# Keys and the sample's queries of a retention layer turned by VectorE blocks and DMAs instead of TensorE, in a two-layer streaming encoder

## The reference

```
z = rmsnorm(h) @ w_in                  -> u | gp | q | k | v | gr, 1024 columns each
qr = rotary(q) ; kr = rotary(k) / 16   (4 heads of 256)
per chunk: scores = qr @ kr.T * D
           o = scores @ v + (qr * q_decay) @ S
           S = S * chunk_decay + (kr * k_decay).T @ v
o = groupnorm(o) * g_gn * silu(gr)
h = h + concat(pool(u) * silu(gp), o) @ w_out
h = h + sigmoid(rmsnorm(h) @ w_pg) * (p @ w_ple) ; at the end rmsnorm(h)
```

## Time and profile before

| | us |
|---|---|
| median of 3 runs | 2436.83 |
| lowest, highest | 2434.78, 2438.3 |
| the profiled execution's own time | 2435.57 |
| its span | 2433.8 |
| PE busy in it | 2419.9 |
| DVE busy | 1059.6 |
| ACT busy | 635.7 |
| POOL busy | 300.0 |
| mean granted TensorE clock, share of full speed | 0.998 |

### The profile page before, as it was taken

How to read it: one execution, slowest core, us unless ns; L and a number is a source line. 1 busy time by engine, 2 the same in 40 slices (tenths; PEclk the granted TensorE clock), 3 DMA queues, 4 the chain that set the end, 5 groups by cost and what they waited for, 6 DMA issues and landing times.

```text
span 2433.8 us, 27213 instructions
## 1 busy us (share of the span) xinstructions
PE 2419.9 (99%) x11024; PEld 1994.5 (82%) x11024; DVE 1059.6 (44%) x1650; ACT 635.7 (26%) x994; POOL 300.0 (12%) x471
## 2 busy tenths in 40 slices
PE   9999999999999999999999999999999999999998
PEld 8888888888888888888888888888888888888886
DVE  6343443444455335444543433434434552354445
ACT  6212221221233223322432122122122231242222
POOL 2102102103112001000020120120130120010001
PEclk9999999999999999999999999999999999999999
DMA  7344244244244334223342442442442454332323
GB/s 233 99 124 137 81 131 136 81 123 152 86 130 155 109 100 128 81 76 120 103 160 78 134 135 78 124 137 87 118 154 80 131 162 122 109 112 78 95 70 113
DMA packets 187566, 283.73 MB, mean 117 GB/s; under 512 B 19024, under 2 KB 130960, under 8 KB 186160
## 3 DMA queue, kind: packets, MB, share of 16 engines
q1 hardware_dynamic: 143616, 173.05, 23.7%
q0 software_dynamic: 29824, 95.11, 12.5%
q10 hardware_dynamic: 14000, 13.83, 2.4%
HBM read 235.45 MB, written 46.46 MB: 116 GB/s over the span
## 4 chain that ended last, share of the span: by engine, by line
PE 98%; DVE 1%; DMA 0%; ACT 0%; issue 0%; SPq 0%; POOL 0%; DVEq 0%; POOLq 0%; ACTq 0%
PE acc L1567 89%; PE side L1567 8%; PE osb L1794 1%; DMA Z<-in_x_t 0%; PE side L1757 0%; DVE Wlo L971 0%; PE osb L1567 0%; DVE Z L1415 0%; DVE Alo L974 0%; PE side L1683 0%; DVE HT L1408 0%; DVE HT L1527 0%; PE side L1730 0%; ACT Ahi L618 0%; DVE HS L1408 0%
## 5 line engine op out<-in xcount | busy, mean ns | idle before, releaser
L1567 PE MATMUL acc<-Ahi,Whi 128*128 128x512 f32 x2016 | 794.5, 394 | 1.2 <-DVE Wlo L971 1.2
L1567 PE MATMUL acc<-Alo,Whi 128*128 128x512 f32 x2016 | 784.8, 390 | 0.0
L1567 PE MATMUL acc<-Ahi,Wlo 128*128 128x512 f32 x2016 | 784.5, 389 | 0.0
L597 ACT ACTIVATE Whi<-raw 128x1024 fp32r<-128x1024 f32 x315 | 333.5, 1059 | 1509.4 <-PE acc L1567 1484.6
L971 DVE TENSOR_TENSOR Wlo<-raw,Whi 128x1024 fp32r<-128x1024 f32 x315 | 384.8, 1222 | 751.4 <-ACT Whi L597 750.9
L1567 PE MATMUL acc<-Whi,Ahi 128*128 128x512 f32 x1144 | 448.3, 392 | 0.0
L1567 PEld LDWEIGHTS acc<-Ahi,Whi 128*128 128x128 f32 x2016 | 378.5, 188 | 84.2 <-issue 4.3
L1567 PE MATMUL acc<-Whi,Alo 128*128 128x512 f32 x1144 | 445.5, 389 | 0.0
L1567 PE MATMUL acc<-Wlo,Ahi 128*128 128x512 f32 x1144 | 445.0, 389 | 0.0
L1567 PEld LDWEIGHTS acc<-Alo,Whi 128*128 128x128 f32 x2016 | 378.4, 188 | 79.3
L1567 PEld LDWEIGHTS acc<-Ahi,Wlo 128*128 128x128 f32 x2016 | 378.7, 188 | 78.8 <-issue 1.0
(11 more groups left out here) (217 smaller groups left out, 1577.3 us busy)
## 6 DMA issues: line engine op xcount, KB each, us to landing
raw<-in_w_in SPq DMA_DIRECT2D x384, 256.0 KB, 3.1
raw<-in_w_out SPq DMA_DIRECT2D x128, 256.0 KB, 3.3
raw<-in_w_pg SPq DMA_DIRECT2D x128, 256.0 KB, 3.2
Ss<-in_state_ret POOLq DMA_DIRECT2D x64, 256.0 KB, 4.8
out_new_ret_sample<-Ss POOLq DMA_DIRECT2D x64, 256.0 KB, 3.1
kv_parts<-stage ACTq DMA_DIRECT2D x16, 256.0 KB, 2.4
turned_o<-XF POOLq DMA_DIRECT2D x32, 128.0 KB, 3.4
XF<-turned_o POOLq DMA_DIRECT2D x8, 512.0 KB, 4.1
```

The lines of the kernel that those rows point to most:

```text
L597: nc.scalar.activation(w_parts(m)[0], raw[:, p % 2], ACT.Copy).then_inc(w_hi, 1)
L1567: return nc.tensor.matmul(out, lhsT, rhs, start=start, stop=stop)
```

## The change

Neither keys nor the sample's queries are turned by TensorE any more. In step 9 of `kv` DVE transposes the sample's rotated queries in 32x32 blocks into `SV[:, 0]` (`SV` is `Sp` and `vd` joined in one tensor); POOL writes them to DRAM in 4 DMAs and reads them back into `qT` (`exchange_queries`). In steps 0 to 2 of `gt` DVE transposes each rotated tile of keys in blocks, the prompt's four into `SV`, the sample's into `ST`; POOL writes and reads them in the same way (`exchange_keys`). The prompt's four tiles are interleaved in `SV`, `turned_k` and `kT`: token t of a tile stands four elements behind token t - 1, and the stationary operand of the prompt's scores is read at that step. The scores come one step later (prompt in step 6, sample in 7), the first state update between them, the sample's part into `osb` in step 8. ACT writes the first two `vd` in step 5 instead of 0, after `k_written`, and spreads the sample's queries in steps 14 and 15. Four copies of DVE for each head are gone.

More of the change, by code:

```diff
@@ L201, in build @@
         gr = sb("gr", [P, NT])
+        Sp, vd = SV[:, 0:2], SV[:, 2:4]
         tA, tB = ST[:, 0:2], ST[:, 2:4]
@@ L260, in build @@
         turnO = nc.dram_tensor("turned_o", [8, QD, 4, P], F32, kind="Internal").ap()
+        turnK = nc.dram_tensor("turned_k", [8, QD, 4, P], F32, kind="Internal").ap()
+        turnQs = nc.dram_tensor("turned_qs", [8, QD, 4, QD], F32, kind="Internal").ap()
+        turnKs = nc.dram_tensor("turned_ks", [8, QD, 4, QD], F32, kind="Internal").ap()
         tables, settled, zeroed = sem("tables"), sem("settled"), sem("zeroed")
@@ L274, in build @@
         o_turned, o_written, o_back, o_taken = (sem(n) for n in ("o_turned", "o_written", "o_back", "o_taken"))
+        k_turned, k_written, k_back = sem("k_turned"), sem("k_written"), sem("k_back")
+        ks_turned, ks_written, ks_back = sem("ks_turned"), sem("ks_written"), sem("ks_back")
+        qs_turned, qs_written, qs_back = sem("qs_turned"), sem("qs_written"), sem("qs_back")
         sq_done, sq_added, ssq_done = sem("sq_done"), sem("sq_added"), sem("ssq_done")
@@ L489, in _ @@
                             .then_inc(x_zeroed, 16)
+                    exchange_queries(hh)
+                    exchange_keys(hh)
                     if h == HEADS - 1:
@@ L714, in kv_jobs @@
                             spread_q(0)
-                        if s == 14:
+                        if s == 15:
                             spread_q(1)
@@ L720, in kv_and_gates @@
                     ac.wait_ge(q_rot, hh + 1)
-                    ac.wait_ge(side_ready, ready("qs", l, h))
+                    ac.wait_ge(qs_turned, hh + 1)
                     ac.wait_ge(upool_out, (hh + 1) * UPOOL)
@@ L1224, in kv_jobs @@
                         if s == 9:
-                            evac(("qs", l, h), copy(qT[:, :, NP:TOK]))
+                            ve.wait_ge(rot_done, hh * (NT + 1) + 1)
+                            nc.vector.transpose(qs_src, Z[:, NPT, DH:NW].rearrange("p (g b) -> p g b", g=8)) \
+                                .then_inc(qs_turned, 1)
                     stream(q, kv_jobs)
@@ L1278, in gate_jobs @@
                             rotate(hh * (NT + 1) + 1 + t, t, 0, q)
-                        if s == 3:
-                            evac(("k", l, h, 0), copy(kT[:, 0, 0:NP]))
-                            evac(("k", l, h, 1), copy(kT[:, 1, 0:NP]))
+                            ve.wait_ge(rot_done, hh * (NT + 1) + 2 + t)
+                            if t == 0:
+                                ve.wait_ge(qs_written, 64 * (hh + 1))
+                            out, turned = (k_src[:, :, t], k_turned) if t < NPT else (ks_src, ks_turned)
+                            nc.vector.transpose(out, Z[:, t, 0:DH].rearrange("p (g b) -> p g b", g=8)) \
+                                .then_inc(turned, 1)
                         if s == 4:
-                            evac(("k", l, h, 2), copy(kT[:, :, NP:TOK]))
                             ve.wait_ge(kv_split, hh * 2 + 1)
@@ L1289, in gate_jobs @@
                                                     kv_hi[:, DH:NW].bitcast(F32), ALU.subtract).then_inc(kv_split, 1)
-                        if s == 5:
+                        if s == 6:
+                            ve.wait_ge(ks_written, 64 * (hh + 1))
                             evac(("sc", l, h, 0), lambda bank: nc.vector.tensor_tensor(
@@ L1293, in gate_jobs @@
                                 head[:, C_MASKP:C_MASKP + P].unsqueeze(1).to_broadcast([P, NPT, P]), ALU.mult))
-                        if s == 6:
+                            update(0)
+                        if s == 7:
                             evac(("sc", l, h, 1), lambda bank: nc.vector.tensor_tensor(
@@ L1725, in pool_map @@
                         last.then_inc(side_ready, 1)
[L1727 to L1732, removed]
                     def kv_jobs(s):
@@ L1746, in kv_jobs @@
                             pool_map(2)
-                        if s == 9:
-                            pe.wait_ge(rot_done, hh * (NT + 1) + 1)
-                            turn_queries()
                     stream(q, kv_jobs)
[L1753 to L1759, removed]
                     def scores(i, tiles):
@@ L1810, in gate_jobs @@
                     def gate_jobs(s):
-                        if s == 3:
+                        if s == 6:
+                            pe.wait_ge(q_rot, hh + 1)
+                            pe.wait_ge(k_back, 16 * (hh + 1))
+                            scores(0, range(NPT))
                             pe.wait_ge(rot_done, hh * (NT + 1) + NT + 1)
[L1813 to L1822, removed]
+                            update(0)
+                        if s == 7:
+                            pe.wait_ge(qs_back, 16 * (hh + 1))
+                            pe.wait_ge(ks_back, 16 * (hh + 1))
                             scores(1, (NPT,))
@@ L1825, in gate_jobs @@
                             output(0)
-                        if s == 7:
-                            update(0)
+                        if s == 8:
                             pe.wait_ge(side_free, freed("sc", l, h, 1))
```

5 lines of the change are left out of this document (1 added, 4 removed).

## The result

The changed kernel takes 2451.91 us (median of 6 runs, 2449.19 to 2456.4) against 2436.82 us before: ratio 1.0066, 95% interval 1.0055 to 1.0076. It is 15 us slower. The forecast was 2426.0, the range ended at 2441. The profiled execution has a span of 2449.9 us, 16.1 more than before. Of all runs behind this text one stands apart: one of the nine of the last but one experiment (VectorE's writes without the step) took 5505.6 us, and the record shows no cause.

What follows compares the result with a forecast made beforehand. TensorE was taken to bound the kernel; 10.9 us of transposes leave it and all else is costed at 0, so 2435.57 - 10.9 = 2424.7 us for the profiled execution, 2426.0 as median. Range 2424 to 2441 us.

Steps and rivals of the forecast that it cites:

- What bounds the kernel: TensorE, busy for 99% of the span: each instruction leaving its queue shortens the kernel, each wait put there lengthens it.
- The transposes at 0.11 us each, 10.9 us in all: Key and query transposes leaving TensorE's queue save 1.37 us a head, 10.9 us for 8 heads.
- The order costed at 0: Scores, first update and first output regrouped on TensorE: 0, with 0.8 us in all either way.
- The stepped operand taken at 0: Prompt's scores load keys at a step of four fp32: no cost taken, upper bound 13.4 us in all.
- The wait on k_back costed at 0: TensorE's wait for turned keys in step 6: keys arrive 0.8 to 3.5 us ahead, so no cost.
- rival B: Keys come late at TensorE's wait in step 6: say 2.5 us a head, 20 us, 2446; chance 0.13.
- A: Stepped load in the prompt's scores is slower: at half rate 13.4 us more, 2439.4; chance 0.30.

Runs made afterwards that it cites:

- s2_nokv: Kernel with keys interleaved in pairs (step of two), ACT's four DMAs of the sample's k and v parts left out in all heads but the first: 2426.82 us.
- s2_dfirst: Kernel with keys interleaved in pairs (step of two), reordered: first state update ahead of the prompt's scores in step 6: 2424.86 us.
- b_queries: Kernel before, with only the sample's queries turned by VectorE block transpose and DMAs, the keys left to TensorE: 2434.32 us.
- a_dfirst: Changed kernel, stepped loads kept, with the first state update put ahead of the prompt's scores in step 6: 2442.86 us.
- a_plain: Changed kernel, with the prompt's scores reading their stationary operand without a step (order of the keys then wrong): 2433.4 us.

## Why the prediction was wrong, point by point

**What bounds the kernel.** Right. TensorE is the path, and in s2_nokv and s2_dfirst the time followed its queue.

**The transposes at 0.11 us each, 10.9 us in all.** Right as far as the runs can tell: in the kernel with pairs and the reordering the span is 8.8 us shorter with 2.2 us still lost in step 6, its median 11.0 us lower, and b_queries gives 1.5 of 1.9, within noise.

**The order costed at 0.** Right for the chosen steps: outside step 6 no group changed by more than 0.1 us. But the order held a cover that I did not look for: the first update could stand ahead of the wait.

**The stepped operand taken at 0.** This is the first step that failed. Its upper end, 13.4 us by the loads' pitch doubling, was nearly right: measured are 14.0 us alone, and 1.83 us a head or 14.6 in all in the loads. I had seen in the earlier trace rows that the load sets the pace of the scores, so that any slowing would reach the path; then I took the contiguous rows as the nearest, though they could not tell anything on the question. Where a row can't speak, the choice of 0 was a guess. The Trainium skill, SBUF — State Buffer, section "Door 1: The DMA port swizzle", has the rule that this case bears out: two hits on a 16-byte line are wanted. A step of two fp32 is free here, a step of four costs 0.11 us a load and 0.19 us a block transpose. Its sentence that four fp32 can be stepped for free doesn't hold here. Only steps of one, two and four were run.

**The wait on k_back costed at 0.** The second step that failed. Most of its terms held, on the second head's clock: POOL's first DMA came 0.8 us after the transposes, the read was issued 5.7 us after that (5.2 to 6.8 were forecast, and the eight heads show 5.6 to 7.3), and TensorE's date was 20.1 us after DVE's start (20.1). Two terms were short. The transposes took 0.64 and not 0.42 us, and the last ended 7.3 us after DVE's start instead of 6.8. And the read took 5.8 to 7.9 us to land, median 7.2, not 3.9 to 5.0. I had taken it from the outputs' read, which has the same size but stands alone in its stretch, while the keys' read runs beside ACT's writes of the k and v parts. The prediction had both dates and did not lay them side by side: it moved ACT's writes to about 324.8 and had the read issued between 323.7 and 325.3. Both terms lay in rival B, which priced 2.5 us of lateness a head; measured are 1.05 on average.

**The clock.** No case had it. Behind three of eight waits, of 1.0 to 1.8 us, the granted clock fell to 0.50, and that added 1.1 us each. The stepped loads had a part in it (see a_dfirst).

**The cases taken as alternatives.** The third failure, and the one that put the result outside the range. A and B were priced one at a time, at 2439.4 and 2446, and the range was cut at 2441. They don't exclude each other: both came, and they share a cause, since one step of four elements slowed TensorE's load and the writes that the keys wait for. Added to the forecast, 2426.0 + 14.6 + 8.4 + 4.6 = 2453.6 us, 1.7 above what was measured.

## What to carry to other kernels

Before work is taken from the bounding engine, look at what the new layout does to the operands that stay there: a step of 16 bytes in a small product's stationary operand cost more here than the transposes that it saved. Take the time to land from a transfer that runs beside the same other transfers, not from one of the same size elsewhere, and put an independent product of the bounding engine ahead of the wait. Where two unknown costs come from one edit, add them up for the range.

## What the runs showed of the hardware that I had not expected

The 16 stepped loads take 3.81 us both while the granted clock is at its upper level (334.94 on) and in the first head, where it falls to 0.50 before they end. The 16 contiguous loads of a_plain do follow the clock: 1.86 us at the upper level, 3.43 us in the fifth head, where it is at 0.50 while they run. So the read of SBUF, and not TensorE's clock, seems to set the pace of the stepped ones; this was not tested by itself. A wait of 1.0 us let the clock fall in one head, while 1.1 us did not in two others, and with loads at full pace 2.2 us did not, so the length of the wait alone does not decide it here.
